# adaLN modulation with the condition vectors stationary, and a transpose back to columns

## The reference, cut to what matters

```python
def adaln(cond, w_ada, b_ada):
    m = jnp.einsum('bd,de->be', jax.nn.silu(cond), w_ada) + b_ada
    return jnp.split(m[:, None, :], 6, axis=-1)
...
sh1, sc1, g1, sh2, sc2, g2 = adaln(c, w_ada[l], b_ada[l])
h = modulate(rms_norm(x, norm1_g[l]), sh1, sc1)
q, k, v, u = mixer_inputs(h, w_in[l], q_norm_g[l], k_norm_g[l])
attn = neighbourhood_attention(q, k, v, cache_k[:, l], cache_v[:, l], rpb[l])
pool = multiscale_pool(u, w_pool[l], pool_scale[l])
x = x + g1 * merge_project(attn, pool, out_norm_attn_g[l], out_norm_pool_g[l], w_out[l])
h = modulate(rms_norm(x, norm2_g[l]), sh2, sc2)
x = x + g2 * swiglu(h, w_gate[l], w_up[l], w_down[l])
```

## Time and profile before

| | |
|---|---|
| median of 2 runs | 1654.21 us (1651.82 to 1656.59) |
| the profiled execution's own time | 1651.59 us |
| its span on core 7 | 1650.0 us (the eight cores: 1624.8 to 1650.0) |
| TensorE busy, weight loads busy | 1276.2 us, 743.0 us |
| VectorE, ScalarE, GpSimd busy | 274.0, 238.1, 309.2 us |
| packets of the POOL DMA queue | 379808, 146.29 MB |

### The profile page before, as it was taken

The page is one execution under the profiler, slowest core; times in us unless marked ns, Lnnn a source line. Parts: engine busy times, 40 slices in busy tenths (PEclk is TensorE's granted clock), DMA queues, the critical chain, the costliest instruction groups (busy, mean ns, idle before and its releaser), DMA issues.

```text
span 1650.0 us, 20664 instructions; the slowest of 8 cores (1624.8 to 1650.0 us)
## 1 busy us (share of the span) xinstructions
PE 1276.2 (77%) x8040; PEld 743.0 (45%) x8040; DVE 274.0 (17%) x708; ACT 238.1 (14%) x494; POOL 309.2 (19%) x278
## 2 busy tenths in 40 slices
PE   0201489777888544759949898899999999999997
PEld 0201475333444333545427455556666666444443
DVE  0000236300015234342113000000000002000000
ACT  0100533211112322510023000000000001000000
POOL 1001021111110110402331232222222210131231
PEclk9655699888998667868979899999999998899999
DMA  9999999999997991292991999999999973487882
GB/s 246 195 155 153 112 91 120 110 124 128 111 107 81 142 82 39 79 196 68 117 103 18 122 115 125 122 117 101 102 102 103 103 77 51 66 139 103 140 140 53
DMA packets 390703, 183.82 MB, mean 111 GB/s; under 512 B 315984, under 2 KB 380880, under 8 KB 388560
## 3 DMA queue, kind: packets, MB, share of 16 engines
q0 software_dynamic: 379808, 146.29, 82.7%
q1 hardware_dynamic: 10800, 36.21, 6.4%
HBM read 318.27 MB, written 10.49 MB: 199 GB/s over the span
## 4 chain that ended last, share of the span: by engine, by line
PE 58%; DMA 27%; DVE 4%; issue 4%; ACT 2%; POOL 2%; another core or an unknown queue 1%; SPq 0%; DVEq 0%; POOLq 0%; ACTq 0%
PE bank L295 57%; DMA wada<-w_ada 24%; DMA xa<-ck 3%; POOL x L308 1%; DVE ycatT L321 1%; PE bank L299 1%; DVE sqbuf L308 1%; ACT junk L536 1%; DVE scr L308 1%; DVE tmpS L321 1%; ACT Es L303 0%; DVE junkh L323 0%; DVE qst L308 0%; ACT junkA L536 0%
## 5 line engine op out<-in xcount | busy, mean ns | idle before, releaser
L295 PE MATMUL bank<-h2T,wg 128*128 128x512 bf16 (+1 forms) x1408 | 243.4, 332 | 0.0
L295 PE MATMUL bank<-h2T,wu 128*128 128x512 bf16 (+1 forms) x1408 | 236.0, 326 | 0.0
L295 PE MATMUL bank<-winr,hT 128*128 128x512 bf16 x992 | 234.5, 395 | 0.0
L295 PE MATMUL bank<-wdr,aT 128*128 128x512 bf16 x1056 | 231.4, 381 | 1.3 <-DVE scr L308 1.3
L295 PE MATMUL bank<-sT,wada 128*128 128x2 bf16 x1536 | 50.0, 164 | 210.4 <-DMA wada<-w_ada 209.3
L291 POOL DMA_DIRECT2D wada<-w_ada x72 | 82.5, 1146 | 539.2 <-PE bank L295 450.9
L295 PEld LDWEIGHTS bank<-h2T,wg 128*128 128x128 bf16 x1408 | 138.9, 99 | 93.9 <-issue 6.9
L295 PEld LDWEIGHTS bank<-h2T,wu 128*128 128x128 bf16 x1408 | 137.8, 98 | 91.0
L295 PEld LDWEIGHTS bank<-wdr,aT 128*128 128x128 bf16 x1056 | 103.7, 98 | 128.7 <-issue 7.0
L295 PEld LDWEIGHTS bank<-winr,hT 128*128 128x128 bf16 x992 | 99.0, 101 | 117.3 <-issue 17.8
L295 PEld LDWEIGHTS bank<-sT,wada 128*128 128x128 bf16 x1536 | 48.3, 100 | 228.0 <-issue 221.5
(11 more groups left out here) (89 smaller groups left out, 816.0 us busy)
## 6 DMA issues: line engine op xcount, KB each, us to landing
wada<-w_ada POOLq DMA_DIRECT2D x64, 512.0 KB, 10.7
wg<-w_gate POOLq DMA_DIRECT2D x44, 512.0 KB, 10.7
wu<-w_up POOLq DMA_DIRECT2D x44, 512.0 KB, 10.2
wdr<-w_down POOLq DMA_DIRECT2D x44, 512.0 KB, 5.7
wada<-w_ada POOLq DMA_DIRECT2D x8, 2048.0 KB, 47.2
winr<-w_in POOLq DMA_DIRECT2D x8, 2048.0 KB, 26.7
woutr<-w_out POOLq DMA_DIRECT2D x4, 2048.0 KB, 19.3
xa<-xs SPq DMA_DIRECT2D x5, 1024.0 KB, 25.4
```

Source lines behind the costliest of these rows:

```text
L295: return P.add("pe", lambda e: e.matmul(o, lhsT=l, rhs=r, start=start, stop=stop), reads=[lhsT, rhs], writes=[out])
```

## The change

1. The 64 steps of one j become 32 steps of two j (b from 16 to 47). A load is 256 columns, 1 MB on chip, 512 bytes per row of the matrix; there are still two buffers, now 8 KB per partition each instead of 4.
2. In a step `sT` (2 columns) is the stationary operand and the weights (128 x 256) are the moving one: 16 matmuls give 2 x 256 in a bank of the rotation. ScalarE copies that to `mrow`. Two transposes put it back as columns in `bmod`.
3. A barrier on TensorE stands ahead of the 16 matmuls and behind the two transposes: the next TensorE instruction waits until the one before it has completed, by semaphore.
4. Steps are called half as often or less: every 12th norm group, every 4th projection group (up to 18 in all), every third round of `run_gens` (up to 24), and then in f = 0 to 7.
5. Room is made: `NFR` is 4 instead of 5; `diagA`, `invs`, `wpool` and `tmpS` get other addresses. The load of `invs` moves from ahead of the attention stage to behind that of `maskneg`. `wpool` now lies where `winr` lay, so its load waits for the end of the projection.

```diff
+    def pe_barrier(self):
+        self.pe_fence = True
...
+        if eng == "pe":
+            if self.pe_fence and self.last_pe is not None:
+                op.deps.add(self.last_pe)
+                op.force.add(self.last_pe)
+                self.pe_fence = False
+            self.last_pe = op
...
+    mrow = [const(f"mrow{i}", [128, 256], F32) for i in range(2)]
...
-    wada2 = [Tens(P, f"wada2_{i}", [128, 16, 128], BF16, off=(198 + 4 * i) * KB) for i in range(NW2)]
+    wada2 = [Tens(P, f"wada2_{i}", [128, 16, 256], BF16, off=(190 + 8 * i) * KB) for i in range(NW2)]
...
-    NFR = 5
+    NFR = 4
...
-        for j in range(32, 32 + NW2):
-            ld(j)
-        for j in range(32, 96):
-            wsl = wada2[(j - 32) % NW2]
+        def ld(b):
+            dma("pool", wada2[b % NW2][:, :, :], wada_v[:, :, b * 256:(b + 1) * 256], f"wada2_{b % NW2}")
+        for b in range(16, 16 + NW2):
+            ld(b)
+        for b in range(16, 48):
+            wsl = wada2[b % NW2]
+            bk = P.next_bank()
+            P.pe_barrier()
             for c in range(NCH):
-                mm(bmod[:, j * 2:(j + 1) * 2], wsl[:, c, :], sT[:, c, :], c == 0, c == NCH - 1)
-            if j + NW2 < 96:
-                ld(j + NW2)
-            if j == 47:
+                mm(bk[0:2, 0:256], sT[:, c, :], wsl[:, c, :], c == 0, c == NCH - 1)
+            if b + NW2 < 48:
+                ld(b + NW2)
+            mr = mrow[b % 2]
+            act(mr[0:2, :], bk[0:2, 0:256], AF.Copy)
+            for k in range(2):
+                j = 2 * b + k
+                tr(bmod[:, j * 2:(j + 1) * 2], mr[0:2, k * 128:(k + 1) * 128], ident[0:2, 0:2])
+            P.pe_barrier()
...
-            if n_idx == 0 and evi[0] % 6 == 0:
+            if n_idx == 0 and evi[0] % 12 == 0:
...
-            if nstep[0] < 36 and bgrp[0] % 2 == 0:
+            if nstep[0] < 18 and bgrp[0] % 4 == 0:
...
-            if nstep[0] < 48:
+            rnd[0] += 1
+            if nstep[0] < 24 and rnd[0] % 3 == 0:
```

More of the change, by code:

```diff
@@ L25 @@
 class Op:
-    __slots__ = ("eng", "kind", "fn", "deps", "signal", "ev", "waits", "key", "idx", "small")
+    __slots__ = ("eng", "kind", "fn", "deps", "signal", "ev", "waits", "key", "idx", "small", "force")
 class View:
@@ L153, in add @@
         op.idx = len(self.ops)
+        op.force = set()
         self._record(op, reads, writes)
         op.deps |= set(extra)
+        if eng == "pe":
[4 more added lines that the diff above has]
+            self.last_pe = op
         self.ops.append(op)
@@ L159 @@
     rot = 8
+    pe_fence = False
+    last_pe = None
+    def pe_barrier(self):
+        self.pe_fence = True
     def next_bank(self):
@@ L169, in emit @@
             for d in op.deps:
-                if d.kind == "dma" or d.eng != op.eng or d.small or op.eng != "pe":
+                if d.kind == "dma" or d.eng != op.eng or d.small or op.eng != "pe" or d in op.force:
                     d.signal = True
@@ L189, in emit @@
             for d in op.deps:
-                if d.kind != "dma" and d.eng == op.eng and not d.small and op.eng == "pe":
+                if d.kind != "dma" and d.eng == op.eng and not d.small and op.eng == "pe" and d not in op.force:
                     continue
@@ L407, in build_program @@
     junkA = Tens(P, "junkA", [128, D], BF16, off=112 * KB)
-    diagA = [Tens(P, f"diagA_{i}", [128, 128], F32, off=186 * KB + 512 * i) for i in range(9)]
+    diagA = [Tens(P, f"diagA_{i}", [128, 128], F32, off=150 * KB + 512 * i) for i in range(8)]
+    diagA.append(Tens(P, "diagA_8", [128, 128], F32, off=186 * KB))
     attn_g2 = Tens(P, "attn_g2", [128, 8, 256], F32, off=32 * KB)
@@ L424, in build_program @@
     Ap = Tens(P, "Ap", [128, 2, 4, 256], BF16, off=176 * KB)
-    invs = Tens(P, "invs", [128, 4, 256], F32, off=180 * KB)
+    invs = Tens(P, "invs", [128, 4, 256], F32, off=176 * KB)
     invp = Tens(P, "invp", [128, 4, 256], F32, off=184 * KB)
-    wpool = Tens(P, "wpool", [128, 4, 2, 256], BF16, off=188 * KB)
-    tmpS = Tens(P, "tmpS", [128, 512], F32, off=192 * KB)
+    wpool = Tens(P, "wpool", [128, 4, 2, 256], BF16, off=180 * KB)
+    tmpS = Tens(P, "tmpS", [128, 512], F32, off=184 * KB)
     h2T = Tens(P, "h2T", [128, 16, 768], BF16, off=134 * KB)
     gbc2 = Tens(P, "gbc2", [128, 2, D], F32, off=134 * KB)
-    NFR = 5
+    NFR = 4
     ffr = [(Tens(P, f"wg{i}", [128, 16, 128], BF16, off=(158 + 8 * i) * KB),
@@ L498, in ada2_gen @@
     def ada2_gen():
-        def ld(j):
-            dma("pool", wada2[(j - 32) % NW2][:, :, :], wada_v[:, :, j * 128:(j + 1) * 128],
-                f"wada2_{(j - 32) % NW2}")
-        for j in range(32, 32 + NW2):
-            ld(j)
-        for j in range(32, 96):
-            wsl = wada2[(j - 32) % NW2]
-            for c in range(NCH):
-                mm(bmod[:, j * 2:(j + 1) * 2], wsl[:, c, :], sT[:, c, :], c == 0, c == NCH - 1)
-            if j + NW2 < 96:
-                ld(j + NW2)
-            if j == 47:
+        def ld(b):
[6 more added lines that the diff above has]
+            P.pe_barrier()
+            for c in range(NCH):
+                mm(bk[0:2, 0:256], sT[:, c, :], wsl[:, c, :], c == 0, c == NCH - 1)
[7 more added lines that the diff above has]
+            P.pe_barrier()
+            if b == 23:
                 mod_evac(32, 48)
-            elif j == 79:
+            elif b == 39:
                 mod_evac(48, 80)
                 make_gs(1, 64, C_N2G)
-            elif j == 95:
+            elif b == 47:
                 mod_evac(80, 96)
@@ L653, in build_program @@
     dma("sp", Ap[:, :, :, :], Ap_d[:, :, :, :], "c_Ap")
-    dma("sp", invs[:, :, :], invs_d[:, :, :], "c_invs")
     dma("sp", invp[:, :, :], invp_d[:, :, :], "c_invp")
@@ L766, in build_program @@
     bufs = [(attn_g, pool_g), (attn_g2, pool_g2), (attn_g, pool_g)]
+    rnd = [0]
     def run_gens(alive):
@@ L782, in build_program @@
     dma("sp", maskneg[:, :, :], mask_d[:, :, :], "c_mask")
+    dma("sp", invs[:, :, :], invs_d[:, :, :], "c_invs")
     run_gens([attn_gen(2, attn_g), pool_gen(2, pool_g)])
     run_gens([merge_gen(2, attn_g, pool_g)])
-    while nstep[0] < 48:
+    while nstep[0] < 24:
         ada2_step()
@@ L855, in build_program @@
         dumps.append(("dbg_gbc1", flat(gbc1[:, :, :]), [128, 2 * D], F32))
+        dumps.append(("dbg_modT", flat(modT[:, :, :]), [128, 192], F32))
         return finish(kv_stores)
```

## The result

| | before | after |
|---|---|---|
| median of the runs, us | 1655.72 (10 runs) | 1619.55 (11 runs) |
| ratio, 95% interval | | 0.9766 [0.9734, 0.9798] |
| profiled execution, slowest core, us | 1650.0 (core 7) | 1615.7 (core 1) |
| core 7, us | 1650.0 | 1602.4 |

The kernel became faster, by 2.3%. Forecast and measurement are 7 us apart (1627 and 1619.55), but that nearness is partly luck, as the stages and core 7 show: the forecast was worked out on core 7, which fell by 47.6 us and not by 27. Ratios compare only runs in which no die was slowed, and of e3, whose profiled run was 1.7% above its fastest, only the output stage is used (126.4).

What follows compares the result with a forecast made beforehand. TensorE's work and its waits for loads were taken to set the end. Stage terms +1.6 - 21 - 11 + 3 = -27.4 us against 1651.6 give 1624.2, forecast as a median of 1627; 8-in-10 range 1594 to 1664.

Steps and rivals of the forecast that it cites:

- The step: Each of 32 swapped steps takes 3.34 us, 2.52 more than two old ones: 81 us of new TensorE time (70 to 99).
- The projection: Input projection falls from 306.5 to 285 us, with 5 us of waits left: net -21 (0 to -27).
- The queue hardly gets faster. What doubles is the lead: Loads of `w_ada`: 7.9 us for one wide against 8.7 for two narrow; issued two steps ahead, each four groups instead of two.
- the 512-byte packet: DMA price of a wide load's packets, taken as 3.85 ns each (3.65 to 4.24), so 2048 take 7.9 us.
- The attention: Attention stage: first call net -16, two more steps in the second call +5, together about -11 us (-3 to -20).
- The first call: First call of `run_gens` falls from 55 to 39 us: 18.6 besides steps and waits, four steps 19, waits 1 to 2.
- The output stage: Output projection and second norm: no change counted; the other edits, `NFR` 4 among them, were taken to cost nothing.
- The norm stage: Norm stage: steps add 10.1 us, 12.5 of waits and 1.7 of clock go, 4 and 1.7 remain: net +1.6.
- The feed-forward: f = 0 to 15 go from 202 to 205 us, with 12 of waits and clock remaining: net +3 (-8 to +15).
- The clock falls at the steps: Rival: each step drops TensorE's clock to 1.2 GHz, slowing its matmuls and the next group; some 92 us, about 1715; chance 0.10.
- The waits stay: Rival: loads still land late in a binding queue, in projection, feed-forward and attention; 1663 us at worst, about 1650 middle; chance 0.22.
- All the waits go: Rival: no waits, clock up through attention, step 3.0 us; projection 280, feed-forward 191, total about 1598 us; chance 0.23.

Runs made afterwards that it cites:

- e3: The kernel before with all five buffer pairs, the fifth pair of feed-forward weight loads issued two blocks later: 1649.25 us, ratio 0.994 to before.
- e1: The kernel after with its 256-column loads, but weights stationary again, without copy, transposes or barriers: 1553.23 us, ratio 0.942 to the kernel before.
- e4: The kernel before with only the operands swapped: 64 steps of 128 columns, each with barriers, one copy and one transpose: 1710.88 us, ratio 1.0302.
- e5: The kernel after without the two barriers of a step: 1607.61 us, ratio 0.9726 to the kernel before.
- e6: The kernel after without barriers and with a step's transposes made one step later: 1610.38 us, ratio 0.9698 to the kernel before.
- e12: The kernel after with weights stationary again, wide loads issued one step ahead instead of two: 1588.72 us, ratio 0.9609 to the kernel before.
- e2: The kernel before with `NFR` 4 instead of 5 and nothing else: 1644.11 us, ratio 0.9934.

## Why the prediction was right, and where it was not

**The whole** was right within 7 us, and by luck in part. The forecast took core 7 as it was and added -27.4, to 1624.2; that core ended at 1602.4. The slowest core of after is another one, core 1, at 1615.7. Its prologue, which the change leaves alone, took 181.6 us where the median is 167.8. So the slowest core's time fell by 34.3 where core 7's fell by 47.6.

**The step** was right: 3.34 forecast, 3.23 to 3.56 measured with a median of 3.34, and the swap was rightly taken for pure cost. e1 shows it on the whole kernel (66 us), e4 by itself (3%). The terms of 0.1 for a semaphore, 0.05 and 0.2 for the weight loads had no row behind them; what the runs show is that the two barriers together cost 0.44 (e5) and the round trip by ScalarE 0.66 (e6).

**The projection** was right in its work: 214 + 12 + 7 + 14 x 3.34 = 279.8, with no wait instead of the 5 that I left; core 7 has 278.6. From that core's 306.6 it is -28.0 and not -21; the medians' -20.5 starts from 299.0. Its reason was half right. "The queue hardly gets faster. What doubles is the lead" failed at e12, where the old lead with wide loads did nearly as well (255 us against 249). One term under it is wrong: the 512-byte packet. On core 7 of after, in 870:940, with the DMA engines busy throughout, the packets are

```profile
DMA packets 28276, 9.52 MB, mean 136 GB/s; under 512 B 19335, under 2 KB 28273, under 8 KB 28273
```

As an estimate, with 2.12 ns for each of the 19335 small ones (the price in the earlier trace rows), the 8938 others took (70000 - 40990) / 8938 = 3.25 ns; core 1 gives 3.58 in the same way. I took 3.85 with a low bound of 3.65. By that a wide load is 6.7 to 7.3 us instead of 7.9, against 8.7 for two narrow ones. The line of the Trainium skill in the prediction (DMA: Bandwidth & Descriptors, Specifications, 512 B as the least for line rate) pointed to this side, and the trace goes further than its low end. That wide steps also place the loads otherwise in relation to `winr` may add to it; no run separates that.

**The attention** came out at -11 forecast and -17.4 in the medians. On core 7 it is -11.4, because this core's attention before, 208.0, was 3.8 us below the median; but inside it the terms were mis-sized. The first call, from its first matmul to the end of its last step, took 33.9 us on core 7, not 39. The step of the prediction that failed is "ScalarE alone needs 14.8, so it can't shrink much further", by which 18.6 of rounds were added to 19 of steps and the waits. The timeline of core 7 has the four steps:

```profile
525.62 2.15 PE L307 MATMUL bank<-wada,sT 128*2 128x256 bf16 x16 [0.26 <-PE bank L307]
532.51 1.91 PE L307 MATMUL bank<-wada,sT 128*2 128x256 bf16 x16 [0.25 <-DVE attn_g L320]
544.40 3.57 PE L307 MATMUL bank<-wada,sT 128*2 128x256 bf16 x16 [6.18 <-DMA wada<-w_ada]
551.27 2.95 PE L307 MATMUL bank<-wada,sT 128*2 128x256 bf16 x16 [0.33 <-DMA wada<-w_ada]
```

To the matmul behind them they take 3.4, 3.2, 4.7 and 4.3, 15.6 in all; the first two run at or near the full clock. With the wait of 6.2, 12.1 us are left for the rounds, less than ScalarE's 14.8: ScalarE works on under the steps and the wait, so its time is a floor for the whole call and not for the rest of it. The rounds shrank because the clock rose: the same four rows of a round take 1.26 us here (529.91 to 531.17) and took 2.29 in the kernel before (556.17 to 558.46). So rounds came out 6.5 below the forecast, steps 3.4 below, and waits some 5 above. The second call cost +8.3 (52.1 to 60.4) where I had +5.

**The output stage** was missed: "The other edits cost nothing that I can find" looked at what `NFR` 4 might lose and not at what it frees. It gives 8 of the 38 us (10.2 on core 7), through POOL's blocked issues, as e2, e3 and the traces show together.

**The norm stage**: +2.2 for +1.6, but with another content. The wait that I put down to the load is gone on core 7, and TensorE now waits 6.3 us a little later for the evacuation of its banks:

```profile
200.92 6.78 PE L307 MATMUL bank<-diagA,xa 128*128 128x128 f32 x40 [6.28 <-DVE hT L327]
```

VectorE and ScalarE are still at the statistics then: the first evacuation starts at 199.55. In the kernel before it starts at 197.93, only 1.4 us ahead of the end of the old wait. So most of the old wait was theirs too, and it was named after the load because that ended last.

**The feed-forward** was right: f = 0 to 15 take 201.2 and 205.0 us on cores 7 and 1 (205 forecast), the whole stage +4.5 by the medians for +3, and -2.2 on core 7.

**The rivals.** "The clock falls at the steps" is refuted in the stretch where it would have cost most. Core 7, feed-forward:

```profile
860.27 5.36 PE L307 MATMUL bank<-h2T,wg 128*128 128x512 bf16 x32 [0.26 <-PE bank L311]
...
930.19 3.57 PE L307 MATMUL bank<-wada,sT 128*2 128x256 bf16 x16 [4.19 <-DMA wada<-w_ada]
934.86 7.46 PE L307 MATMUL bank<-h2T,wg 128*128 128x512 bf16 x32
```

Behind a step without a wait, 32 matmuls take 5.36, the full-clock time of the earlier trace rows; only behind the wait of 4.19 do they take 7.46. "The waits stay" fell with 10.7 of 112 us left on core 7. "All the waits go" described the projection well and the rest less. That nothing is gained by the swap itself is what e1 and e4 show.

So by the medians the forecast's size came about through an output stage too high by 8 and an attention too high by 6, while the feed-forward, the norm and the prologue came out 3 us dearer together. By core 7 it is the projection (7), the output stage (10) and the feed-forward (5), and the longer prologue of core 1 hid some 9 of it. The measured before was also 1.5 us longer than the one I started from. The bigger thing that the prediction did not say is that its own two numbers, +81 for the swap and up to -112 for the waits, belong to parts that can be had apart.

## What to carry to other kernels

Where a change buys the end of a wait with more work on the engine that sets the end, split it in two: here all that surrounds the swap, mainly the wider loads and the longer lead, gave 102 us (e1), and the swapped operands cost 66. Never cost an edit that touches an in-order queue by its bytes alone: look at which computing instructions stand behind the issues on the same engine. Compare a forecast with the core that it was worked out on, and not only with the slowest one. An engine's busy time is a floor for a whole stretch, and whatever is added to the stretch can run over it.

## What the runs showed of the hardware that was not expected

In e6, core 6 has a dense stretch of the projection, 64 matmuls with no wait among them, at a granted clock of 0.81, and the same work 75 us later at 1.00. The two windows:

```profile
342.00:359.00 17.00, 16.71 (x64) 6.86 (x64) 0.69 (x1) 2.64 (x5) 1.14 (x1) 0.81 1.10 164
417.00:431.00 14.00, 13.79 (x65) 6.24 (x67) 0.00 (x0) 2.64 (x5) 1.14 (x1) 1.00 1.16 158
```

Both windows have the same work on ScalarE and POOL and nearly the same traffic, and TensorE had been busy ahead of both. In the projection cores 6 and 7 show it and the others don't. In the feed-forward it is cores 0, 1, 4 and 5: all four stand at 0.81 from about 900 us to about 1055, with few waits. Core 0 and then core 2, which doesn't show it, in the same window:

```profile
950.00:1050.00 100.00, 99.11 (x500) 55.22 (x508) 8.16 (x16) 6.98 (x16) 18.29 (x16) 0.81 0.88 83
950.00:1050.00 100.00, 100.00 (x618) 60.22 (x616) 9.17 (x18) 8.72 (x20) 22.30 (x20) 1.00 1.10 101
```

Both are busy throughout, with 500 matmuls in one and 618 in the other. No other kernel's profiled execution has such a long stretch at 0.81. So a clock below full is not always the trace of a wait; its cause here is open.

A swapped step in which TensorE multiplies two columns of weights for 1.9 us, waits 0.61 and transposes leaves the clock at full speed on either side: in the projection of core 7 it is 1.00 over 278.6 us with 14 such steps.
